# Two-layer diffusion backbone in float32: normed tokens parked in device memory, rotations one turn later, rotary keys in two zero-padded copies

## The reference

```python
for l in range(DEPTH):                       # DEPTH = 2
    h = h + 0.5 * m[:, 2] * swiglu(modulate(h, m[:, 0], m[:, 1]), w_ff1_in[l], w_ff1_out[l])
    u = modulate(h, m[:, 3], m[:, 4])        # rms_norm(h) * (1 + scale) + shift
    y = even_mixer(u, ...) if l % 2 == 0 else odd_mixer(u, ...)
    h = h + m[:, 5] * y
    h = h + 0.5 * m[:, 8] * swiglu(modulate(h, m[:, 6], m[:, 7]), w_ff2_in[l], w_ff2_out[l])
```

```python
z, xbc, dtr, qa, ckv, kr = jnp.split(t @ w_in, E_SPLITS, axis=-1)    # t = u
kn, v = jnp.split((rms_norm(ckv, kv_norm) @ w_kvb)..., [128], axis=-1)      # 8 heads
qn, qr = jnp.split((rms_norm(qa, qa_norm) @ w_qb)..., [128], axis=-1)       # qr: 64 wide
s = (jnp.einsum("bqhd,bkhd->bhqk", qn, kn)                            # 128 numbers a head
     + jnp.einsum("bqhd,bkd->bhqk", rope(qr), rope(kr))) * scale      # 64, one key for all heads
o = softmax(s) @ v
y = concatenate([ssd_merge(...), o]) @ w_out
```

## Time and profile before

| | us |
|---|---|
| median of three runs | 3781.41 (3775.68 to 3782.12) |
| the profiled execution | 3775.05 |
| its span | 3773.0 |
| PE busy in it | 3472.1 (92%) |
| DVE busy | 1679.5 (45%) |
| ACT busy | 997.0 (26%) |
| POOL busy | 204.5 (5%) |

### The profile page before, as it was taken

One profiled execution on the slowest core, in us unless ns is written; L12 is line 12 of the kernel. 1 busy time (PEld: TensorE's weight loads), 2 busy tenths in 40 slices (PEclk: granted clock), 3 DMA queues, 4 the chain that ended last, 5 costly groups with the idle time before them and its releaser, 6 DMA issues.

```text
span 3773.0 us, 44929 instructions
## 1 busy us (share of the span) xinstructions
PE 3472.1 (92%) x18399; PEld 3063.4 (81%) x18399; DVE 1679.5 (45%) x2568; ACT 997.0 (26%) x1493; POOL 204.5 (5%) x248
## 2 busy tenths in 40 slices
PE   4999999988986998888999999999999778889999
PEld 3999999775566895468999998999999656667887
DVE  5735533334432536655626323742222437744333
ACT  2211111463331321133212112211211425533222
POOL 0100000000000005520000000100000000000000
PEclk8999999999998998999999999999999989999999
DMA  4534421111001220003525221432222210013333
GB/s 159 164 93 129 128 87 55 42 33 34 1 12 32 57 63 1 1 23 95 156 68 150 72 62 56 151 90 62 67 58 60 45 39 1 1 45 88 94 93 94
DMA packets 385439, 260.35 MB, mean 69 GB/s; under 512 B 33410, under 2 KB 365433, under 8 KB 385145
## 3 DMA queue, kind: packets, MB, share of 16 engines
q1 hardware_dynamic: 364537, 182.50, 16.8%
q0 software_dynamic: 20736, 75.51, 6.4%
HBM read 255.87 MB, written 2.10 MB: 68 GB/s over the span
## 4 chain that ended last, share of the span: by engine, by line
PE 49%; DVE 5%; ACT 2%; issue 2%; POOL 1%; DMA 0%; ACTq 0%; DVEq 0%; POOLq 0%
PE ps L440 43%; PE ps L1096 1%; DVE stat L1155 1%; PE ps L597 1%; PE ps L1114 1%; DVE hid_f L528 1%; DVE u_lo L539 1%; PE ps L506 1%; PE ps L1468 1%; DVE w_lo L430 1%; PE ps L1105 0%; PE ps L986 0%; ACT prob L1125 0%; DVE ps L1151 0%; DMA m_in<-in_w_mod 0%
## 5 line engine op out<-in xcount | busy, mean ns | idle before, releaser
L440 PE MATMUL ps<-u_hi,w_hi 128*128 128x384 f32 (+2 forms) x2992 | 841.6, 351 | 106.4 <-DVE u_lo L539 49.3
L430 DVE TENSOR_TENSOR w_lo<-ring,w_hi 128x1024 fp32r<-128x1024 f32 (+3 forms) x357 | 415.5, 1166 | 960.0 <-ACT w_hi L415 773.1
L440 PE MATMUL ps<-u_lo,w_hi 128*128 128x384 f32 (+2 forms) x2992 | 832.0, 348 | 0.0
L440 PE MATMUL ps<-u_hi,w_lo 128*128 128x384 f32 (+2 forms) x2992 | 830.5, 347 | 0.0
L440 PEld LDWEIGHTS ps<-u_hi,w_hi 128*128 128x128 f32 x2992 | 544.9, 192 | 157.0 <-issue 92.0
L440 PEld LDWEIGHTS ps<-u_hi,w_lo 128*128 128x128 f32 x2992 | 548.8, 192 | 22.8
L440 PEld LDWEIGHTS ps<-u_lo,w_hi 128*128 128x128 f32 x2992 | 549.2, 192 | 21.9
L415 ACT CAST w_hi<-ring 128x1024 fp32r<-128x1024 f32 (+3 forms) x229 | 221.9, 970 | 1212.0 <-PE ps L440 1159.1
L440 PE MATMUL ps<-hid_hi,w_hi 128*128 128x384 f32 (+1 forms) x1232 | 345.7, 350 | 0.0
L440 PE MATMUL ps<-hid_lo,w_hi 128*128 128x384 f32 (+1 forms) x1232 | 344.9, 350 | 0.0
L440 PE MATMUL ps<-hid_hi,w_lo 128*128 128x384 f32 (+1 forms) x1232 | 344.2, 349 | 0.0
(11 more groups left out here) (236 smaller groups left out, 3704.9 us busy)
## 6 DMA issues: line engine op xcount, KB each, us to landing
ring<-in_w_ff_in SPq DMA_DIRECT2D x176, 512.0 KB, 3.9
m_in<-in_w_mod POOLq DMA_DIRECT2D x128, 512.0 KB, 4.0
ring<-in_w_ff_out SPq DMA_DIRECT2D x64, 512.0 KB, 3.8
ring<-in_w_in_e SPq DMA_DIRECT2D x26, 512.0 KB, 3.8
ring<-in_w_ff_out SPq DMA_DIRECT2D x32, 384.0 KB, 3.3
m_first<-in_w_mod POOLq DMA_DIRECT2D x16, 512.0 KB, 12.1
ring<-in_w_out_e SPq DMA_DIRECT2D x16, 512.0 KB, 3.9
ring<-in_w_in_o SPq DMA_DIRECT2D x16, 256.0 KB, 3.5
```

Of the source, the lines that this page charges most:

```text
L430: dve.tensor_tensor(w_lo[:, b:b + WIDE[n]], ring[:, s:s + WIDE[n]], w_hi[:, b:b + WIDE[n]], ALU.subtract).then_inc(w_split_lo, 1)
L440: mm = pe.matmul(ps_at(p, c0, c1) if halved else pair(p)[:, c0:c1], w, x[:, c0:c1], start=start and i == 0, stop=stop and i == 2)
```

## The change

It has three parts.

1. **Normed tokens wait in device memory.** `pool_keep` writes each block of `u_hi` and `u_lo` (16 transfers of 128 x 768 float32, 384 KB each) to a buffer in device memory as soon as it is made. The first write over them waits for all of these: `kn`'s first raw write on ACT, `vt`'s on DVE. `pool_fetch` reads them back once the attention's last output is done, and the first product of `pe_proj` waits for it. The second norming goes.
2. **Rotations one turn later.** `dve_items` runs the three rotation instructions of item m after the split and the norming of item m+1. Their temporary gets a place of its own, `rope_t`, and ACT no longer waits for the rotation before it reuses `rsh`.
3. **Rotary keys laid out twice.** Besides `kr` there is `kr1`: `kr` keeps the keys in partitions 0 to 63 and zeros below, `kr1` has zeros above and the keys in partitions 64 to 127. The rotary products run over 128 rows, with `kr` or `kr1` by the head's parity. Also, both `qn` pieces of a unit now come before both `qr` pieces.

```diff
+        kr1, rope_t = at("kr1", 36 * T, T), at("rope_t", H0 + 6 * T, SEQ)
...
+        kept = nc.dram_tensor("kept_u", (2, DB, P, T), F32R, kind="Internal").ap()
...
+        def pool_keep(pool):
+            for d in range(DB):
+                pool.wait_ge(n_lo, 8 * NORM_RUN[1] + d + 1)
+                for e, x in enumerate((u_hi, u_lo)):
+                    pool.dma_start(kept[e, d], x[:, d, :]).then_inc(u_kept, 16)
+        def pool_fetch(pool):
+            pool.wait_ge(u_kept, 32 * DB)
+            pool.wait_ge(at_o, n_mla)
+            for d in range(DB):
+                for e, x in enumerate((u_hi, u_lo)):
+                    pool.dma_start(x[:, d, :], kept[e, d]).then_inc(u_back, 16)
...
@@ act_items
+                    if it["kind"] == "kn" and it["i"] == 0:
+                        act.wait_ge(u_kept, 32 * DB)
...
-                        last = [x for x in items if x["stop"]][nn - 2]
-                        if last["rope"]:
-                            act.wait_ge(hn_fin, last["nrope"] + 1)
@@ dve_items
-            for m in range(m0, m1):
-                it = items[m]
-                dve_split(dve, base + m - m0 + 2)
...
+            for m in range(m0, m1 + 1):
+                if m < m1:
+                    dve_split(dve, base + m - m0 + 2)
+                    if items[m]["stop"]:
+                        dve_head_norm(dve, m)
+                if m > m0 and items[m - 1]["rope"]:
+                    dve_rope(dve, items[m - 1])
...
+        def dve_rope(dve, it):
+            nr = it["nrope"]
+            d, tmp = dst_of(it)[:, 0:SEQ], rope_t[:, :]
+            dve.wait_ge(hn_rp, nr + 1)
+            if nr:
+                dve.wait_ge(hn_fin, nr)
+            dve.tensor_tensor(tmp, cst[:, C_SIN:C_SIN + SEQ], bank(6), ALU.mult).then_inc(hn_sin, 1)
+            dve.tensor_tensor(d, d, cst[:, C_COS:C_COS + SEQ], ALU.mult).then_inc(hn_cos, 1)
+            dve.wait_ge(hn_sin, nr + 1)
+            dve.wait_ge(hn_cos, nr + 1)
+            x = dve.tensor_tensor(d, d, tmp, ALU.add)
+            x.then_inc(hn_fin, 1)
+            if it["kind"] == "kr":
+                dve.memset(kr1[0:64, :], 0.0).then_inc(kr_two, 1)
+                dve.wait_ge(hn_fin, nr + 1)
+                dve.tensor_copy(kr1[64:128, :], kr[64:128, :]).then_inc(kr_two, 1)
+                dve.wait_ge(kr_two, 2)
+                dve.memset(kr[64:128, :], 0.0).then_inc(kr_two, 1)
@@ units of the first attention
-                for k0, k1 in keys:
-                    sco.append((qn[:, hh, q0:q0 + P], kn[:, hh, k0:k1], at, True, False))
-                    sco.append((qr[e:e + 64, hh // 2, q0:q0 + P], kr[e:e + 64, k0:k1], at, False, True))
-                    at += k1 - k0
+                for part in range(2):
+                    for k0, k1 in keys:
+                        lhs, rhs = ((qn[:, hh, q0:q0 + P], kn[:, hh, k0:k1]),
+                                    (qr[:, hh // 2, q0:q0 + P], (kr, kr1)[hh % 2][:, k0:k1]))[part]
+                        sco.append((lhs, rhs, k0 - keys[0][0], part == 0, part == 1))
@@ pe_proj
+                if q == 0:
+                    pe.wait_ge(u_back, 32 * DB)
                 for k in range(DB):
-                    if q == 0:
-                        pe.wait_ge(n_lo, 8 * AGAIN + k + 1)
@@ act_mla_out, dve_mla_out
-                act_shift(act, 1, AGAIN, d)
...
-            for d in range(DB + 1):
-                if d < DB:
-                    dve_split(dve, b + d + 2)
-                    dve_scale(dve, 1, AGAIN, d)
-                if d > 0:
-                    dve_low(dve, 1, AGAIN, d - 1)
-                    dve_residual(dve, R_MLA, d - 1)
+            for d in range(DB):
+                dve_split(dve, b + d + 2)
+                dve_residual(dve, R_MLA, d)
```

More of the change, by code:

```diff
@@ L456, in build @@
         NORM_T = [T, T, T, T, T, SEQ]
-        NORM_RUN, AGAIN = [0, 1, 3, 4, 5, 6], 2
+        NORM_RUN = range(6)
         NEXT = [("ffi", 0, 0), "even", ("ffi", 1, 0), ("ffi", 2, 0), "odd", ("ffi", 3, 0)]
@@ new lines, in dve_items, with dve_head_norm @@
+            for m in range(m0, m1 + 1):
[5 more added lines that the diff above has]
+                    dve_rope(dve, items[m - 1])
+        def dve_head_norm(dve, m):
+            it = items[m]
+            t, nn, kind = it["t"], it["norm"], it["kind"]
+            dve.wait_ge(hn_rs, nn + 1)
+            dve.wait_ge(hn_raw, m + 1)
+            for i in range(it["i"] + 1 if kind in ("qa", "ckv") else 1):
+                d = DST[kind][:, i, :t] if kind in ("qa", "ckv") else dst_of(it)[:, :t]
+                x = dve.tensor_tensor(d, d, rsh[:, nn % 2, :t], ALU.mult)
+            x.then_inc(hn_n, 1)
+            if kind in ("qa", "ckv"):
+                dve.wait_ge(hn_hi, nn + 1)
+                full, hi, lo = (qa, qa_hi, qa_lo) if kind == "qa" else (ckv, ckv_hi, ckv_lo)
+                for i in range(it["i"] + 1):
+                    x = dve.tensor_tensor(lo[:, i, :], full[:, i, :], hi[:, i, :], ALU.subtract)
+                x.then_inc(hn_lo, 1)
```

34 lines of the change are left out of this document (8 added, 26 removed).

## The result

The changed kernel takes 3651.93 us (median of 4 runs, 3647.24 to 3653.36) where the kernel before, on the same chip, takes 3781.76 (4 runs, 3775.68 to 3786.81): 129.8 us less, a ratio of 0.9655 with a 95% interval of 0.9638 to 0.9672. The prediction said 3648, with 3630 to 3684 as its range.

What follows compares the result with a forecast made beforehand. TensorE, busy 92% of the span, bounds the kernel; its waits, lower clock and overlong products can be won. 54.5 + 49.5 + 25.6 = 129.6 us off 3775.05 gives 3645.5, put at 3648 for the median, range 3630 to 3684.

Steps and rivals of the forecast that it cites:

- product d+1 never waits for more than update d-1: First attention's output projection: update d follows split d+2, so eight products take 67.0 us; stretch 70.9, gain 54.5 us.
- The fetch and the keeping: 16 transfers of 384 KB each way, hidden under 67 us of products and at least 50 us of items: no cost.
- The rival of late tokens: Parked-token transfers slower than thought, to or from device memory; past 7.7 us each the whole gain is lost; chance 0.07.
- The turn: Second layer's query items, rotation one turn later: 7.37 us without a wait in place of 13.3, seven turns gaining 41.5 us.
- DVE's slack: Second layer's turn: DVE's split ends at 7.6 us, TensorE needs it at 9.1, so 1.5 us slack and no wait.
- a wait costs as much again in clock: Second layer's turns: 3.4 us idle makes a turn 13.3 in place of 7.4, the lower clock costing as much again.
- The lower bound of this part: Rotations one turn later, both layers: gain 49.5 us, with bounds given as 37 to 58.
- `kr`'s turn: First layer's key rotation: the rotation wait goes, a split wait after it comes; even, bounds -3 and +3 us.
- Four changes ... each 0.2 us: First attention: four changes between 64 and 128 rows in each of 32 latent units, 25.6 us gained.
- The lower bound of 18: First attention's gain in us if latent units run into ACT's `probT` copy in every second unit.
- The context units: First attention: ACT's copy to `probT` ends last there, so shorter scores gain nothing; 31 us in all if they gain too.
- The Trainium skill's rule: First attention: 128-row weight loads would not be hidden, total 25.6 us less; within the attention-without-gain rival, 3674 us, chance 0.09.

Runs made afterwards that it cites:

- four rounds of sixteen: The changed kernel, fetching the 16 parked pieces four times over, one round after the other, with the next projection waiting for the last: 3671.3 us.
- the part undone: The changed kernel with rotary products over 64 rows in the old order, without `kr1` and the three DVE instructions that make it: 3671.7 us.
- padding: The changed kernel with the second attention's keys also standing twice with zeros, so its score products have 128 rows: 3644.4 us.
- ACT's new order: ACT copies `probT` ahead of its exponential in both attentions, against the kernel with padded keys, `kr` work on GpSimd and an earlier projection start: 3612.2 us.

## Why the prediction was right

*The output projection.* The step "product d+1 never waits for more than update d-1" holds turn by turn: one wait is left where seven stood, and the eight products take 66.8 us for the 67.0 foreseen. The runs add that the gain's cause was the place of one instruction: 50 of the stretch's 54.9 us come without any parking.

*The fetch and the keeping.* Costed at nothing, and nothing they cost: TensorE waits for no transfer back, and ACT for none ahead of `kn`. But the working was too cautious: one transfer after the other at 3.0 us each was to take 48 us; all sixteen took 22, while the DMA engines moved 331 GB/s, SP's weight blocks included. The rival of late tokens with its 7.7 us a transfer was far away: four rounds of sixteen took 88 us, 1.4 a transfer. The Trainium skill warns ("SBUF — State Buffer", SBUF: two separate sides) that GpSimd's transfers can starve for descriptors while DVE runs an operation in its two-port mode, such as a float32 copy within SBUF. Nothing of the kind showed: in four rounds the DMA engines moved 326 GB/s beside DVE's 18.6 us of work, with issues 0.52 us apart within a round, but for one that came 1.1 us late. DVE is busy a quarter of that time, with splits and updates and no such copy, so the case that the page describes remains untested here.

*The rotations.* The turn was put at 7.37 us and is 7.21. DVE's slack, put at 1.5 us, is what decided, and it was there, if smaller: the split ends at 2934.92, and the next product starts behind the swap product, at 2935.95. The prediction said that a wait costs as much again in clock; the two windows above split the 45 us into 26 of waits and 19 of clock. The lower bound of this part does not add up: 35, 2 and the -3 of `kr` give 34 and not 37. The range holds it all the same.

*`kr`'s turn.* Taken as even, and even it is: the wait for the rotation went, one of 3.27 us for the split behind it came, and the stretch is 0.3 us longer. The runs show the two sizes that met: the later rotation alone brings 3.5 us (75.5 to 72.0), the three instructions cost 3.8. That they cancel so closely is luck within bounds of 3 us to either side. Giving the three instructions to GpSimd brings the 3.8 back.

*The attention.* The term was mis-sized, by a tenth: 25.6 foreseen, 23.2 in the traces, both before and with the part undone (the 19.8 by the medians hold `kr`'s 3.8 as well). "Four changes ... each 0.2 us" is wrong for the first of the four, which costs 0.10 (0.09 by the kernel before's own trace). Rows for it stood in the same timeline and were not read. The lower bound of 18, for latent units that run into ACT's copy, was not needed: none does. The context units gained nothing, as foreseen: their scores take 1.31 us to the transposes before and 1.35 after, held by the copy, and 0.86 once ACT copies first. The Trainium skill's rule ("TensorE: Matmul & The Clock Gate", The mechanism) by which a weight load overlaps a running product only where the row groups differ would, as the prediction reads it, have made this part nothing. The same section also lets a load go ahead into a background weight buffer, and that the prediction left out. Here float32 products of 128 rows with new weights each follow each other in 0.86 us at 512 columns, the same as in the scan, and in 0.43 at 256, with loads of 0.19 us for each record; the measurement decides against the narrow reading for products of this size.

*The level.* The prediction's sum, taken off the median of before (3781.4), gives 3651.8, and 3651.9 was measured; the 3.9 us to its 3648 are the choice how far the median would lie above the profiled execution. That the sum is met so closely is partly luck: the 2.4 us missing in the attention are made up by 0.4 more in the output projection and 1.8 more in the rotations, and the medians can't tell differences of this size.

## What to carry to other kernels

Before work is taken away from an engine that another waits for, look at the order in which it stands: here an instruction whose input was long ready stood behind one that waited for the very product it was to make room for, and moving one call up, with one wait more, gave 50 of 55 us. The same question, "what is ready while this engine waits?", found another 24 us in both attentions, in a wait of ACT, an engine that is busy a quarter of the time. And a price taken from one place of a kernel, such as that of a change of rows, is to be read again at the place where it is to be saved: where another engine sets the pace it is nothing. A difference between two traces, before it is divided by the number of units, is to be looked for in time; here it all lay in the first 30 us.

## What the runs showed of the hardware that I had not expected

- A change between float32 products of 64 and of 128 rows cost 0.19 to 0.20 us in three places of a latent unit, 0.10 in the fourth. In the second attention, where DVE and ACT set the pace, padding that left no change made no difference to 192 us of it (178.8 and 178.9 with ACT's new order). What it brought, 2.1 and 4.4 us, came with a clock that was higher at the start: 0.95 in place of 0.79 over some 30 us, and 0.94 in place of 0.74. Why the clock is higher there stays open.
- Sixteen transfers of 384 KB from device memory, issued by GpSimd one behind the other, landed within 22 us. That is 286 GB/s of their own, and 331 with SP's weight blocks, with all DMA engines busy (share 1.03), while TensorE's products beside them keep their pace. A single one's 4.0 us to landing says little of the rate of many.
- GpSimd's copy of 64x768 float32 took 1.09 us in the first layer, where DVE began a split of 0.55 us just before it, and 1.76 in the second, where DVE began one of 1.22. Both copies end 0.67 to 0.69 us after the split beside them, as if they had waited for it; DVE's own copy of that shape took 0.56. Two cases are no proof, and no run settles it.
